# A fused two-layer encoder on one core: the first two experts' rows gathered row-wise with one-hot stationary operands

## What is computed

```
h = rms_norm(x, norm2_g[i])
grp_p, grp_idx = top_k(softmax(h @ w_grp + b_grp), 1)
top_p, top_j = top_k(softmax(the 8 logits of that group), 2)
y[token] += gate * (silu(xr @ w1[e]) * (xr @ w3[e])) @ w2[e]      # for the two experts e of each token
x = x + y
```

## Time and profile before

| | us |
|---|---|
| runs: median of 3 (lowest, highest) | 1572.89 (1572.73, 1574.77) |
| profiled execution: its time, its span | 1576.24, 1574.5 |
| TensorE busy (share of span) | 1346.8 (86%) |
| VectorE, ScalarE, GpSimd busy | 451.3, 325.1, 272.3 |
| HBM over the span | 307 GB/s |
| mean granted TensorE clock | 0.971 of full |

### The profile page before, as it was taken

One profiled execution on the slowest core, in us unless ns is written; L12 is line 12 of the kernel. 1 busy time (PEld: TensorE's weight loads), 2 busy tenths in 40 slices (PEclk: granted clock), 3 DMA queues, 4 the chain that ended last, 5 costly groups with the idle time before them and its releaser, 6 DMA issues.

```text
span 1574.5 us, 21124 instructions
## 1 busy us (share of the span) xinstructions
PE 1346.8 (86%) x8134; PEld 781.2 (50%) x8134; DVE 451.3 (29%) x990; ACT 325.1 (21%) x640; POOL 272.3 (17%) x377
## 2 busy tenths in 40 slices
PE   6998898998777777894999999998998777787893
PEld 3443456565444444462566666556565434444461
DVE  2898445111101010113245444446111010101112
ACT  3565231000000000003244444422000000000000
POOL 3888000122111111110000000000211111111110
PEclk9999899999999999997999999999999999999997
DMA  8513127999999999998401201337999999999996
GB/s 295 166 49 161 54 80 296 420 421 420 425 424 425 423 425 423 396 421 309 183 1 65 97 0 58 157 134 273 421 422 424 424 424 425 424 425 424 382 421 253
DMA packets 72810, 467.23 MB, mean 297 GB/s; under 512 B 16310, under 2 KB 20406, under 8 KB 38952
## 3 DMA queue, kind: packets, MB, share of 16 engines
q1 hardware_dynamic: 60200, 437.38, 67.8%
q0 software_dynamic: 10240, 16.35, 2.8%
q10 hardware_dynamic: 2304, 12.58, 2.0%
HBM read 459.90 MB, written 23.59 MB: 307 GB/s over the span
## 4 chain that ended last, share of the span: by engine, by line
PE 49%; DMA 36%; DVE 7%; POOL 3%; ACT 2%; issue 2%; ACTq 0%; SPq 0%; POOLq 0%; DVEq 0%
DMA ring<-in_moe_w 34%; PE banks L1495 11%; PE banks L1511 11%; PE banks L1628 6%; PE banks L1657 4%; PE banks L1412 4%; POOL scratch L572 2%; DVE banks L963 2%; PE banks L1319 2%; PE banks L1398 2%; PE banks L1717 2%; PE banks L1672 2%; PE banks L1339 1%; DMA area<-y_dram 1%; DMA scratch<-xn_dram,at_in 1%
## 5 line engine op out<-in xcount | busy, mean ns | idle before, releaser
L1495 PE MATMUL banks<-ring,scratch 128*64 128x256 f32 x3904 | 446.5, 384 | 83.8 <-DMA ring<-in_moe_w 74.3
L1495 PEld LDWEIGHTS banks<-ring,scratch 128*64 128x64 f32 x3904 | 299.4, 138 | 248.6 <-DMA ring<-in_moe_w 81.5
L1511 PE MATMUL banks<-ring,scratch 128*64 128x512 f32 x992 | 232.5, 610 | 66.6 <-DMA ring<-in_moe_w 63.4
L1151 DVE COPY scratch<-banks 128x256 f32<-128x256 f32 x66 | 28.0, 425 | 793.7 <-PE banks L1503 793.7
L1511 PEld LDWEIGHTS banks<-ring,scratch 128*64 128x64 f32 x992 | 77.4, 139 | 182.6 <-issue 163.3
L769 ACT ACTIVATE scratch<-banks 128x256 f32<-128x256 f32 x66 | 25.4, 385 | 494.8 <-PE banks L1495 488.4
L1628 PE MATMUL banks<-hT,ring 128*128 128x512 f32 x256 | 120.1, 614 | 0.8 <-DVE hT L917 0.8
L1319 PE MATMUL banks<-hT,ring 128*128 128x512 f32 x256 | 113.2, 602 | 0.8 <-DVE hT L917 0.8
L602 POOL COPY at_out<-rows_out 128x1 int32 (+1 forms) x60 | 11.0, 183 | 590.0 <-ACT scratch L773 590.0
L773 ACT ACTIVATE scratch<-banks 128x512 f32<-128x512 f32 x66 | 39.4, 598 | 348.1 <-PE banks L1511 348.1
L572 POOL TENSOR_TENSOR scratch<-scratch 128x512 f32<-128x512 f32 x77 | 98.0, 1274 | 19.7 <-ACT scratch L736 9.8
(11 more groups left out here) (236 smaller groups left out, 1205.1 us busy)
## 6 DMA issues: line engine op xcount, KB each, us to landing
ring<-in_moe_w SPq DMA_DIRECT2D x178, 2048.0 KB, 26.8
area<-in_moe_w SPq DMA_DIRECT2D x10, 2048.0 KB, 14.4
ring<-in_attn_w_qkv SPq DMA_DIRECT2D x6, 2048.0 KB, 18.7
hT<-in_moe_w SPq DMA_DIRECT2D x4, 2048.0 KB, 17.3
area<-y_dram ACTq DMA_DIRECT2D x8, 1024.0 KB, 7.9
ring<-in_conv_w_in SPq DMA_DIRECT2D x4, 1024.0 KB, 11.4
ring<-in_conv_w_in SPq DMA_DIRECT2D x2, 2048.0 KB, 15.4
ring<-in_conv_w_out SPq DMA_DIRECT2D x2, 2048.0 KB, 23.8
```

Of the source, the lines that this page charges most:

```text
L1495: last = mm(bank[2 + s][q * SLOTS:(q + 1) * SLOTS, k * 256:(k + 1) * 256], xeT[s][:, c % 4, c // 4, :], wc[:, c, q * 256:(q + 1) * 256], s ...
L1511: last = mm(bank[6 + s][q * SLOTS:(q + 1) * SLOTS, :], hidT[s][:, j % 2, j // 2, :], w2c[:, j, q * 512:(q + 1) * 512], start=j == 0, stop= ...
```

## The change

The same two experts' rows are gathered the other way round. `first_rows(l, e, lo, hi)` does one expert: stationary is the 64-column one-hot of one tile, moving are 512 columns of `xn`, in the two column halves of the array, so that the rows come out untransposed in one PSUM bank per expert, laid out like rows that a gather brings. VectorE copies the bank to `xe` (`copy_first`), TensorE transposes it back into the same bank (`first_rows_T`, four 128x128 transposes), and `take_first` multiplies by the gain.

Expert 0's are finished before the turns begin, those of expert 1 between the two halves of expert 0's up matmuls, and transposed between `lists` and `lists2`. `xT_ready` now goes up by 1 for each expert. The zeroing matmuls, `stay_warm`'s matmul between the ranks and the last tiles, and GpSimd's zeroing of `xe` are gone. On SyncE, ring units 6 and 7 go ahead of area1's load. The semaphore `over_y` is merged into `y_stored`, on a path for more than 33 turns that isn't taken in the profile.

```diff
-        hot_first = scratch[:, 1280:1280 + NT * P].rearrange("p (t e s) -> p t e s", t=NT, e=2)
-        first_xT = [banks2[2 * l][:].rearrange("p b (c e k) -> p (b c) e k", e=2, k=SLOTS) for l in range(LAYERS)]
+        hot_first = scratch[:, 1280:1280 + NT * P].rearrange("p (e t s) -> p t e s", t=NT, e=2)
...
+                down_to_ring(6, 2, w1_used, 1)
+                to_ring(7, w1_of(4), up, 1)
                 sp.wait_ge(xn_stored, 16 * NT * (l + 1))
                 to_extra(3, w3_of(3), main[l]["xT_ready"], 2)
-
-                down_to_ring(6, 2, w1_used, 1)
-                to_ring(7, w1_of(4), up, 1)
                 to_ring(8, w3_of(4), w1_used, 2)
...
-                pool.wait_ge(logits_ready, NT * l + 3)
-                for s in range(2):
-                    link(g.memset(xe[s], 0.0))
...
+            def copy_first(l, s):
+
+                dve.wait_ge(first_ready, 2 * l + s + 1)
+                v.tensor_copy(xe[s], first_pair[l][:, s, :]).then_inc(first_copied, 1)
+
             def take_first(l, s):
                 m = main[l]
-                dve.wait_ge(m["xT_ready"], 2)
-                v.tensor_tensor(xeT[s].rearrange("p j h k -> p (j h) k"), first_xT[l][:, :, s, :], gain_jh[N_MOE[l]],
+                dve.wait_ge(m["xT_ready"], s + 1)
+                v.tensor_tensor(xeT[s].rearrange("p j h k -> p (j h) k"),
+                                first_pair[l][:, s, :].rearrange("p (c k) -> p c k", k=SLOTS), gain_jh[N_MOE[l]],
                                 ALU.mult).then_inc(m["xT_taken"], 1)
...
-            def first_rows(l, lo, hi):
-
-                if lo == 0:
-                    for b in range(2):
-                        mm(first_pair[l][:, b, :], zero16[:], ones16[:, 0:1].to_broadcast([P, 512]), start=True, stop=False, skip_group_check=True)
+            def first_rows(l, e, lo, hi):
+
                 pe.wait_ge(xn_done, 4 * N_MOE[l] + hi)
                 pe.wait_ge(hot_first_done, 2 * l + (1 if hi < NT else 2))
+                for t in range(lo, hi):
+                    for q in range(2):
+                        last = mm(first_pair[l][q * SLOTS:(q + 1) * SLOTS, e, :], hot_first[:, t, e, :],
+                                  xn[:, t, q * 512:(q + 1) * 512], start=t == 0, stop=t == NT - 1)
+                if hi == NT:
+                    last.then_inc(first_ready, 1)
+
+            def first_rows_T(l, e):
+
+                pe.wait_ge(first_copied, 2 * l + e + 1)
                 for j in range(4):
-                    for h in range(2):
-                        k = 2 * j + h
-                        for t in range(lo, hi):
-                            last = mm(first_pair[l][:, k // 4, k % 4 * P:(k % 4 + 1) * P], xn[:, t, (4 * h + j) * P:(4 * h + j + 1) * P],
-                                      hot_first[:, t].rearrange("p e s -> p (e s)"), start=False, stop=t == NT - 1,
-                                      skip_group_check=True)
-                if hi == NT:
-                    last.then_inc(main[l]["xT_ready"], 2)
+                    last = nc.tensor.transpose(first_pair[l][:, e, j * P:(j + 1) * P], xe[e][:, j * P:(j + 1) * P], ident[:])
+                last.then_inc(main[l]["xT_ready"], 1)
 
             def route(l):
                 logits(l, NT - 1)
                 pe.wait_ge(x_done, 8 * l + NT)
                 pe.wait_ge(picks_done, NT * l + NT - 1)
-                first_rows(l, 0, NT - 2)
+                first_rows(l, 0, 0, NT - 2)
                 ranks(l, NT - 2, NT)
-                stay_warm(1, warm_bank)
-                first_rows(l, NT - 2, NT)
+                first_rows(l, 1, 0, NT - 2)
+                first_rows(l, 0, NT - 2, NT)
+                first_rows_T(l, 0)
...
-                up_step(0, 0, in_ring(0), in_ring(1))
+                up_step(0, 0, in_ring(0), in_ring(1), lambda: first_rows(l, 1, NT - 2, NT))
                 lists(l)
+                first_rows_T(l, 1)
                 lists2(l)
```

More of the change, by code:

```diff
@@ L164, in trunk @@
         hot_first_done = sem("hot_first_done")
+        first_ready, first_copied = sem("first_ready"), sem("first_copied")
         qk_ready, qk_sq, q_ss, k_ss, q_copied, q_root, k_root, k_done = (
@@ L180, in trunk @@
         over_xe = [sem(f"over_xe{l}") for l in range(LAYERS)]
-        over_y = [sem(f"over_y{l}") for l in range(LAYERS)]
         over_w = [[sem(f"over_w{l}_{k}") for k in range(3)] for l in range(LAYERS)]
@@ L647, in over_scatter @@
                                          in_=y_sb[0], in_offset=None,
-                                         bounds_check=2 * ASSIGN - 1, oob_is_err=False).then_inc(over_y[l], 16)
-                    pool.wait_ge(over_y[l], j * 16 + 16)
+                                         bounds_check=2 * ASSIGN - 1, oob_is_err=False).then_inc(y_stored[l][0], 16)
+                    pool.wait_ge(y_stored[l][0], j * 16 + 16 * (EXPERTS // 2 + 2))
                 pool.wait_ge(ctl_done, l + 1)
@@ L1051, in slots @@
                 link(v.tensor_tensor(place[:, first, :], ranks[:, :, 0:2], miss[:, first, :], ALU.add))
-                v.tensor_tensor(hot_first[:, first].rearrange("p t e s -> p (t e) s"),
-                                iota_slot[:, 0:SLOTS].unsqueeze(1).to_broadcast([P, 2 * n, SLOTS]),
-                                bt(place[:, first, :].rearrange("p t e -> p (t e)"), SLOTS), ALU.is_equal).then_inc(hot_first_done, 1)
+                v.tensor_tensor(hot_first[:, first], iota_slot[:, 0:SLOTS].unsqueeze(1).unsqueeze(1).to_broadcast([P, n, 2, SLOTS]),
+                                place[:, first, :].unsqueeze(3).to_broadcast([P, n, 2, SLOTS]), ALU.is_equal).then_inc(hot_first_done, 1)
                 link(v.tensor_tensor(tmp_kte[:, :, lo:hi, :], picks_kte[:, :, lo:hi, :],
@@ L1070, in route @@
                 v.tensor_tensor(v4(3), v4(5), v4(2), ALU.subtract).then_inc(exp_in, 1)
+                copy_first(l, 0)
                 count = rank_bank[l][:, P:P + EXPERTS]
@@ L1080, in route @@
                 link(v.tensor_reduce(v8(2), eight(tmp2), AX.X, ALU.add))
+                take_first(l, 0)
                 cmp_a = cmp[:, 0:2 * NT * STEPS].rearrange("p (a s) -> p a s", s=STEPS)
@@ L1098, in route @@
                 link(v.scalar_tensor_tensor(v8(5), v8(5), late_is, v8(0), ALU.subtract, ALU.subtract))
-                take_first(l, 0)
                 link(v.scalar_tensor_tensor(v8(5), v8(3), 0.0, v8(5), ALU.is_gt, ALU.mult))
@@ L1104, in route @@
                 v.tensor_tensor(hot_token, hot_tile, bt(token2[:].rearrange("p k t -> p (k t)"), TILES), ALU.mult).then_inc(hot_done, 1)
+                copy_first(l, 1)
                 dve.wait_ge(hot_done, 2 * l + 1)
@@ L1525, in in_extra, with up_step @@
                     return extra_units[k], extra_loaded[k], 16 * ((l + 1) if k == 3 else 2 * l + 1 + again)
-                def up_step(e, s, w1, w3):
+                def up_step(e, s, w1, w3, between=lambda: None):
                     pe.wait_ge(m["xT_taken"], e + 1)
@@ L1531, in up_step @@
                     up(s, 0, w1[0]).then_inc(m["w1_used"], 1)
+                    between()
                     pe.wait_ge(w3[1], w3[2])
```

## The result

The changed kernel takes 1585.22 us (median of 5, 1580.66 to 1587.84), the kernel before 1573.82 in the same comparison. The ratio on record is **1.0064**, interval 1.0054 to 1.0075: some 10 us slower. The two medians alone would give 1.0072, and one of the five executions of before, at 3522.93 us, stands far outside the rest. Measured twice more the changed kernel gave 1.0052 (1.0038 to 1.0065) and 1.0064 (1.0050 to 1.0077). The forecast was 1583.6 us and slower.

What follows compares the result with a forecast made beforehand. The prediction took the full DMA queue's bytes to bound the expert stages. Terms 9.9 + 0.4 + 0.5 = +10.8 us took the profiled 1576.24 to 1587.0, or 1583.6 us against the 1572.89 median; range 1575 to 1589.

Steps and rivals of the forecast that it cites:

- The bound: Expert stages: from the moment the DMA queue is full (424 GB/s), a stage lasts as long as its bytes take.
- X: End of expert 0's first half, which frees ring unit 6; shift put at +0.5 us, bounds -2.7 to +6.5.
- The moved unit: area1's load moves behind ring units 6 and 7 into the full stretch: 4.95 us per layer, +9.9 us.
- Unit 7: Ring unit 7 is issued at X + 5.3 instead of X + 3.4, so the queue runs dry briefly: +0.4 us.
- R: Moment VectorE gets the last ranks (L1050): 1.5 us earlier in layer 0, unchanged in layer 1.
- The sum: Whole kernel: 9.9 + 0.4 + 0.5 = +10.8 us, giving 1583.6 us, 0.7% slower; chance 0.70.
- The covers: Removed memsets, VectorE's second copy, expert 1's later start and the later gather lie within other waits: no cost.
- A: Rival: a later 5 us queue hole per layer absorbs the moved load, X alone counts: faster, 1570.2 us; chance 0.06.
- B: Rival: TensorE's chain, not the queue, sets the stage end: same, +2.5 us, 1575.4 us; chance 0.14.
- C: Rival: first rows and first halves all at 1.2 GHz: X +6.5, in all +16.8, 1589.7 us; chance 0.10.

Runs made afterwards that it cites:

- a: Changed kernel with SyncE's old order, area1's load ahead of ring units 6 and 7, still released by expert 1's transposes: 1595.75 us, 1.0130.
- b: Kernel before with only SyncE's new order, area1's load behind ring units 6 and 7, first rows as before: 1585.44 us, 1.0068.
- c: Changed kernel with expert 1's last first-rows matmuls behind expert 0's transposes, area1's load released by them and ahead of unit 6: 1573.25 us, 0.9994.
- f: Changed kernel with expert 1's last four first-rows matmuls behind the second half of expert 0's up: 1581.96 us, 1.0044.
- d: Changed kernel with two 128x512 matmuls on unused data ahead of the last ranks, in TensorE's wait for the last picks: 1583.14 us, 1.0051.
- m: Changed kernel measured a third time, nothing altered: 1584.17 us, 1.0064.
- g: Changed kernel with area1's load one place later, behind ring unit 8: 1584.33 us, 1.0056.

## Why the prediction came out right, point by point

**The bound.** Right. The stream is full from X on at 423 GB/s, and what is moved out of the hole comes back as time at the end: a, b and c each moved the stream's start or its bytes by a known amount, and the stages followed to 1.3 us or less (12.3 for 13.6 by a's own issues; 9.3 for 9.9; 7.2 for 8).

**The moved unit, +9.9 us.** Right: +9.3 by b's stages, 1.0068 by its runs.

**Unit 7, +0.4 us.** Not distinguishable from nothing (f, and 397 GB/s for 2 us, which is 0.1 us).

**X, +0.5 us.** This step was mis-sized. Its first parts held. R in layer 0 comes 6.4 us after the logits' start instead of 7.9 (1.5 forecast); the copy takes 0.69; the first rows lose 1.7 us (1.6 taken); up starts at R + 8.9, and 7.3 + 1.6 was forecast. But I left expert 0's first half at the pace that it had before, 5.4 and 6.5 us. It ran in 3.7 in both layers of the first profile, and in seven of the twelve stages with this TensorE order. X therefore moved by -2.2 and -1.8 us there, -4.0 in all instead of +0.5, which is outside the bounds that I gave, -2.7 to +6.5; where the half is slow, X comes 20.2 to 20.7 us after the logits' start and moves by less than 1 us. The slow stretch had moved and shrunk: what used to fall on up (1.7 and 2.8 us above 3.7) now fell on the first rows (1.7 each). I counted it in the new place without taking it away in the old one. d shows an exchange between the same two places. That the first rows' slow stretch is what spares up is argued from where the two stood in these profiles; no run shows why, and four of the twelve stages had both slow.

**The sum.** By terms as measured: 9.9 - 4.0 + 0.1 = 6.0 us, and the first profile's stages show 6.4. The runs say more. All 16 executions of the changed kernel have their median at 1583.65 us, and the medians of before in the five comparisons lie at 1573.8 to 1574.9, so +9.2. The profiled executions are not in the middle of their runs: the three of the changed kernel took 1583.80, 1580.24 and 1581.37 us, on average 1.8 below that median, the two of before 1576.24 and 1575.02, 1.1 above theirs. That closes the gap in numbers, not in causes.

The changed kernel's slower executions were those with a lower mean granted clock: the seven above 1584 us have 0.967 to 0.970, the nine others 0.972 to 0.978. The nine have their median at 1581.8 us, which is also the mean of the three profiled ones, all of which are among them. Before has such executions too: 18 of 67 in the later comparisons, with a median 1.8 us above that of the other 49, where the changed kernel's seven lie 3.7 us above its nine. By this split, made afterwards, the change costs 7.6 us at the higher clock and 9.5 at the lower, and the profiles of the changed kernel show only the higher. Slow first halves are one candidate for the difference: with five in twelve stages at some 1.6 us each, the mean execution would be 1.3 us slower than the first profile. That is short of the 2 to 4 us by which the slowest ones lie above it, and none of those was profiled, so the rest stays open.

The forecast of 0.7% thus fits the measurement with a term for X that the profiles don't bear out in its size. That the sum came so close is in part luck, since 4.5 us too much for X stood where the runs have some 3 us that the profiles don't show.

**The covers.** The missing memsets and VectorE's second copy cost nothing that can be measured: c has them and is at 0.9994. Expert 1's start, 6.7 us after X instead of 4.7, and the later gather (expert 2's rows at X + 15.5 in the first profile, 15.2 forecast) are not in c to that extent. That they cost nothing is read from the sum: its terms give 6.0 us and the stages show 6.4. No run tests them alone.

**The rivals.** A (slack further on) is out by a and b. B (TensorE's chain) is out by a, where the units that come late are not needed for many us and the end moved by 12. C, everything at half pace, wasn't seen in a profile. m's layer 1 comes nearest in time, and a's layer 1 and g's layer 0 had a slow stretch in all three blocks (3.0, 5.2 and 5.4 us); even there unit 6's turn, X, came no later than before. The Trainium skill's rule behind it ("TensorE: Matmul & The Clock Gate", Part 1, HAM oscillation) names the danger rightly: slow stretches did stand behind TensorE's waits. They did not stand behind every one: after the 2.2 us wait ahead of up, TensorE ran at full pace in seven stages of twelve.

## What to carry to other kernels

When transfers bound a stage, look at the time before they do: here a load that travelled while the queue was empty was free, and when it left that hole it cost nearly its full transfer time (4.5 and 4.8 of 4.95 us in b), though it landed long before its use. Tie the release of a buffer to its last reader (here the last matmul that reads xn), not to a later step that happens to signal. And when an edit moves TensorE's idle time, count its slow stretch once, at its new place, and take it out of the old.

## What the runs showed of the hardware

Three matmuls on unused data in a 3.2 us wait of TensorE are worth 0.38% of this kernel (k, 0.9962, interval 0.9949 to 0.9975), because up's first half behind the wait ran at full pace and released the weight stream earlier. Two such matmuls in another wait (d) brought nothing, as the granted clock then fell in the next stretch instead: 3.65 and 5.36 us (granted 1.00 and 0.68) in place of 5.35 and 3.67. And a queue that has run dry takes some 2 us to get going: 86 GB/s in the first 2 us from the issue in the changed kernel (82 at the same place before), 172 in a_area_first with area1's unit and unit 6 issued 0.4 us apart, 423 to 425 behind.
